# Folding the squares to one tile on GpSimd and VectorE before TensorE averages them

## The chip, the core and the metric

The kernel runs on one core of a Trainium2 chip. The metric is the time of one execution on the device in microseconds (us), lower is better; for several executions the median is taken. The engines are TensorE (PE for matmuls, PEld for its weight loads), VectorE (DVE), ScalarE (ACT), GpSimd (POOL) and SyncE (SP), which issues the weight transfers. SBUF tiles and PSUM banks have 128 partitions.

## The reference

Two blocks of two layers each run on x of 256 tokens by 2048 features, in fp32. The first block's layers mix by windowed means (layer 0) or by a gated linear recurrence (layer 1), and add a gated embedding. The second block's layers (2 and 3 in the kernel) run three branches: latent attention, a spatial gate, and gated linear attention (gla) with 4 heads of 256 value columns. Every matmul is preceded or followed by a root-mean-square norm; those of x and of each gla head matter here:

```python
def rms_norm(x, g):
    xf = x.astype(jnp.float32)
    y = xf * lax.rsqrt(jnp.mean(xf * xf, axis=-1, keepdims=True) + EPS)
    return (y * g.astype(jnp.float32)).astype(x.dtype)
...
    h = rms_norm(x, norm_g)
    proj = h @ w_in
...
    o = o.transpose(1, 0, 3, 2, 4).reshape(B, S, GLA_HEADS, GLA_DV)
    o = rms_norm(o, o_g).astype(v.dtype)
```

## The kernel before

Activations lie with features on the partitions and the 256 tokens along the free dimension, so a tile of 128 features is 128x256. Weights stream in units of eight 128x128 tiles (512 KB) through four slots. ScalarE rounds a unit to w_hi (L896), VectorE makes the rest w_lo (L1278), and TensorE multiplies w_hi with the high and low part of x (L536, L537) and w_lo with the high part (L544); x is split the same way into xs. In stages "by token" the roles are turned (L566, L574). ScalarE and VectorE prepare a unit three units ahead of TensorE.

The norms are applied late: a stage multiplies un-normed x, and the result is multiplied by rstd. For that the mean of the squares over the features is needed, a sum over partitions. mean_square (L578) has TensorE multiply a constant 128x128 tile mean_d (each value 1/2048) with each tile of squares, one after another into ms_bank, in plain fp32. Behind it ScalarE takes the root (root, L968, with a table load where another function was loaded), VectorE the reciprocal (norm, L1290), and the result scales the products.

Six times x is fed into a stage (the "feeds" 0 to 5: window, gate of layer 0, conv, gate of layer 1, gqk of layer 2, gqk of layer 3). ScalarE squares x in four blocks of 128x1024. GpSimd adds them into sq_sum (4 tiles of 256; sum_squares, L1971). For feeds 0 to 4 it then folds sq_sum from four tiles to two (128x512, L1976). For feed 5 the adds stand in the stage wo of layer 2 (L2109, L2113) without a fold. TensorE averages two tiles (four for feed 5), behind unit 13 or 15 of the feed (mean_of_x).

In layers 2 and 3 the gla heads, the spatial gate and the attention run beside the large stages as side work: generators on each engine that yield the number of a unit, counted from the start of the stage latent, and go on once the engine has come to it. TensorE runs what is yielded as v between the high and the low products of unit v + 1. The other engines run it at unit v, behind the split of the unit three ahead. With scored_at(n) = 4 + 6n, head h has its output made by TensorE at scored_at(2h+2) - 2 (26 for head 1), squared by ScalarE into g_sq (two tiles, L1005) at scored_at(2h+2) - 1, averaged at max(scored_at(2h+2), 20) (20, 28, 40, 52), its root taken at max(scored_at(2h+2) + 1, 21) (21, 29, 41, 53), and normed by VectorE at 22 for head 0, else at min(scored_at(2h+3) - 1, 54) (33, 45, 54). gla_normed, counted there, is waited for by TensorE ahead of the scores of the next head, and by the attention sums at 59.

## Time and profile before

| | before |
|---|---|
| runs, us | 3332.09, 3361.66, 3338.16 |
| median, us | 3338.16 |
| profiled execution, us | 3333.02 |
| its span, us | 3331.2 |
| mean granted TensorE clock | 0.997 |
| TensorE busy | 3310.4 us, 99% |
| VectorE busy | 2290.7 us, 69% |
| ScalarE busy | 1670.7 us, 50% |
| GpSimd busy | 839.1 us, 25% |

The span is the time from the first to the last instruction of the profiled execution; the time of that execution is 1.8 us longer. Busy times are sums of the instructions' spans. Matmuls overlap in the trace, so what one occupies is read from the distance of starts. A timeline merges like instructions that follow each other, and gives the start, the time to the last one's end, the engine, the line, the operation, what it writes and reads, how many, and in brackets the idle time ahead and what ended it.

### The profile page before, as it was taken

How to read it: one execution, taken by the hardware profiler on the slowest of the kernel's cores; microseconds unless marked ns; L12 is line 12 of the kernel's file. 1: busy time of each engine (PE TensorE's matmuls, PEld its weight loads, DVE VectorE, ACT ScalarE, POOL GpSimd, SP SyncE). 2: the span in 40 equal slices, each digit the busy share in tenths (PEclk: the TensorE clock that was granted, in tenths of full speed). 3: DMA queues.
4: the chain of work that ended last, by engine and by line, in shares of the span. 5: the costliest groups of instructions: out<-in, count | busy, mean ns of one | idle time of the engine just before them, and what ended most of it. 6: DMA issues, size and time to landing. Idle time of an engine off the chain costs nothing.

```text
span 3331.2 us, 65552 instructions
## 1 busy us (share of the span) xinstructions
PE 3310.4 (99%) x27820; PEld 3264.4 (98%) x27820; DVE 2290.7 (69%) x3014; ACT 1670.7 (50%) x2108; POOL 839.1 (25%) x807
## 2 busy tenths in 40 slices
PE   9999999999999999999999999999999999999999
PEld 9999999999999999999899999999988999999999
DVE  6986654688888845778878755555567777555554
ACT  5344444555588745555544444444455545444443
POOL 1532320144556500423323200000013232100000
PEclk9999999999999999999999999999999999999999
DMA  6565565556555565555444555555554444555555
GB/s 228 188 203 190 196 224 191 171 173 220 191 181 186 197 224 178 188 172 177 158 165 158 166 192 195 196 192 194 194 179 157 165 151 157 192 191 196 195 192 178
DMA packets 170051, 619.73 MB, mean 186 GB/s; under 512 B 19104, under 2 KB 20768, under 8 KB 169376
## 3 DMA queue, kind: packets, MB, share of 16 engines
q1 hardware_dynamic: 165888, 602.23, 54.6%
q10 hardware_dynamic: 3872, 13.31, 1.1%
q8 instruction: 220, 3.60, 0.4%
q14 instruction: 71, 0.58, 0.1%
HBM read 610.22 MB, written 4.19 MB: 184 GB/s over the span
## 4 chain that ended last, share of the span: by engine, by line
PE 90%; DVE 4%; ACT 4%; issue 1%; DMA 0%; ACTq 0%; SPq 0%; DVEq 0%
PE banks L544 21%; PE banks L536 21%; PE banks L537 21%; PE banks L566 4%; PE pm L544 3%; PE pm L536 3%; PE pm L537 3%; PE banks L574 2%; PE banks L601 2%; PE banks L603 2%; PE banks L608 2%; ACT w_hi L896 2%; DVE w_lo L1278 2%; PE pm L601 1%; PE pm L603 1%; PE pm L608 1%
## 5 line engine op out<-in xcount | busy, mean ns | idle before, releaser
L1278 DVE TENSOR_TENSOR w_lo<-raw,w_hi 128x1024 fp32r<-128x1024 f32 x1144 | 1467.6, 1287 | 868.9 <-ACT w_hi L896 857.0
L896 ACT ACTIVATE w_hi<-raw 128x1024 fp32r<-128x1024 f32 x1144 | 1204.7, 1057 | 974.4 <-PE banks L544 665.6
L536 PE MATMUL banks<-xs,w_hi 128*128 128x256 f32 x4008 | 948.2, 279 | 0.3 <-ACT val L1162 0.3
L537 PE MATMUL banks<-xs,w_hi 128*128 128x256 f32 x4008 | 947.4, 278 | 0.0
L536 PEld LDWEIGHTS banks<-xs,w_hi 128*128 128x128 f32 x4008 | 758.3, 189 | 0.9 <-ACT val L1162 0.7
L537 PEld LDWEIGHTS banks<-xs,w_hi 128*128 128x128 f32 x4008 | 758.3, 189 | 0.2
L544 PE MATMUL banks<-xs,w_lo 128*128 128x256 f32 x4008 | 550.6, 279 | 0.0
L544 PEld LDWEIGHTS banks<-xs,w_lo 128*128 128x128 f32 x4008 | 498.5, 189 | 0.4
L536 PE MATMUL pm<-xs,w_hi 128*128 128x256 f32 x952 | 223.1, 277 | 0.0
L537 PE MATMUL pm<-xs,w_hi 128*128 128x256 f32 x952 | 222.7, 276 | 0.0
L1937 POOL CAST merged<-act 128x256 fp32r<-128x256 f32 x32 | 41.0, 1281 | 714.7 <-DVE act L1717 714.7
L536 PE MATMUL banks<-inner,w_hi 128*128 128x256 f32 x896 | 211.2, 276 | 0.0
L537 PE MATMUL banks<-inner,w_hi 128*128 128x256 f32 x896 | 211.0, 276 | 0.0
L537 PEld LDWEIGHTS pm<-xs,w_hi 128*128 128x128 f32 x952 | 178.9, 188 | 0.1
L536 PE MATMUL banks<-y_abc,w_hi 128*128 128x256 f32 x768 | 178.9, 276 | 0.0
L536 PEld LDWEIGHTS pm<-xs,w_hi 128*128 128x128 f32 x952 | 178.8, 188 | 0.1
L537 PE MATMUL banks<-y_abc,w_hi 128*128 128x256 f32 x768 | 178.8, 276 | 0.0
L537 PEld LDWEIGHTS banks<-inner,w_hi 128*128 128x128 f32 x896 | 168.3, 188 | 0.0
L536 PEld LDWEIGHTS banks<-inner,w_hi 128*128 128x128 f32 x896 | 168.2, 188 | 0.0
L537 PEld LDWEIGHTS banks<-y_abc,w_hi 128*128 128x128 f32 x768 | 144.2, 188 | 0.0
L536 PEld LDWEIGHTS banks<-y_abc,w_hi 128*128 128x128 f32 x768 | 144.2, 188 | 0.0
L1178 ACT ACTIVATE act<-val 128x256 f32<-128x256 f32 x96 | 40.1, 417 | 197.4 <-DVE val L1704 197.4
(336 smaller groups left out, 5922.4 us busy)
## 6 DMA issues: line engine op xcount, KB each, us to landing
raw<-weights SPq DMA_DIRECT2D x1144, 512.0 KB, 3.4
wide<-x_in ACTq DMA_DIRECT2D x4, 512.0 KB, 8.9
wide<-x_in ACTq DMA_DIRECT2D x1, 2048.0 KB, 8.4
x_scratch<-wide ACTq DMA_DIRECT2D x1, 2048.0 KB, 9.1
wide<-x_scratch ACTq DMA_DIRECT2D x1, 2048.0 KB, 10.6
out_x<-wide SPq DMA_DIRECT2D x3, 512.0 KB, 5.3
w_st<-w_s ACTq DMA_DIRECT2D x2, 512.0 KB, 4.2
b_st<-b_s ACTq DMA_DIRECT2D x2, 512.0 KB, 5.6
```

Of the source, the lines that this page charges most:

```text
L536: nc.tensor.matmul(bank, w_hi[:, slot, w], x[:, 0:T], start=(k + t == 0), stop=False)
L537: nc.tensor.matmul(bank, w_hi[:, slot, w], x[:, T:2 * T], start=False, stop=False)
L544: ins = nc.tensor.matmul(bank, w_lo[:, slot, w], p.operand(i, k + t)[:, 0:T], start=False, stop=(k + t == p.depth - 1))
L566: nc.tensor.matmul(product_bank(s, i, j), x[:, at:at + P], w_hi[:, slot, w], start=(k == 0 and at < T), stop=False)
L574: ins = nc.tensor.matmul(product_bank(s, i, j), x[:, j * P:(j + 1) * P], w_lo[:, slot, w], start=False, stop=(k == depth - 1))
L601: nc.tensor.matmul(bank, w_hi[:, slot, w], operand[:, k, 0:T], start=(k == 0 and j < 4), stop=False, skip_group_check=True)
L603: nc.tensor.matmul(bank, w_hi[:, slot, w], operand[:, k, T:2 * T], start=False, stop=False, skip_group_check=True)
L608: ins = nc.tensor.matmul(bank, w_lo[:, slot, w], operand[:, k, 0:T], start=False, stop=(k == s.products[0].depth - 1), skip_group_check=True)
L896: nc.scalar.activation(w_hi[:, slot, :], raw[:, slot, :], ACT.Copy).then_inc(hi_done, 1)
L1178: nc.scalar.activation(act[:, slot, :], val[:, 2 * slot, :], ACT.Tanh, scale=0.5).then_inc(act_ready, 1)
L1278: nc.vector.tensor_tensor(w_lo[:, slot, :], raw[:, slot, :], w_hi[:, slot, :].bitcast(F32), ALU.subtract).then_inc(lo_done, 1)
L1937: link(nc.gpsimd.tensor_copy(dest[:, 0:T], source))
```

## The change

Three edits. On GpSimd a new function fold_squares folds sq_sum from four tiles to two and from two to one, behind the sums of feeds 0 to 4 and now of feed 5 too. On VectorE an add of 128x256 folds the two tiles of g_sq to one for each gla head, at scored_at(2h+2), behind ScalarE's square, and counts gla_folded, for which TensorE waits in place of gla_sq. TensorE averages one tile in all these places. For heads 1 to 3 TensorE's average and ScalarE's root are yielded one unit later than before, and VectorE's norm of head 3 at 55 and not at 54.

```diff
@@ mean_of_x
-                        mean_square(s.layer, which, [sq_sum[:, j, :] for j in range(4 if f == 5 else 2)])
+                        mean_square(s.layer, which, [sq_sum[:, 0, :]])
@@ TensorE gla_results
-                    yield max(scored_at(2 * h + 2), 20)
-                    pe.wait_ge(gla_sq, c * G_HEADS + h + 1)
+                    yield max(scored_at(2 * h + 2) + 1, 20)
+                    pe.wait_ge(gla_folded, c * G_HEADS + h + 1)
                     if h == 1:
                         pe.wait_ge(tok_read, 2 * c + 2)
-                    mean_square(c + 2, f"gla{h}", [g_sq[:, 0, :], g_sq[:, 1, :]])
+                    mean_square(c + 2, f"gla{h}", [g_sq[:, 0, :]])
@@ ScalarE gla_results
-                    yield max(scored_at(2 * h + 2) + 1, 21)
+                    yield max(scored_at(2 * h + 2) + 2, 21)
                     root(c + 2, f"gla{h}", 2 * P, eps128_col)
@@ VectorE gla_results
-                    yield min(scored_at(2 * h + 3) - 1, 54) if h else 22
+                    yield scored_at(2 * h + 2)
+                    ve.wait_ge(gla_sq, c * G_HEADS + h + 1)
+                    nc.vector.tensor_tensor(g_sq[:, 0, :], g_sq[:, 0, :], g_sq[:, 1, :], ALU.add).then_inc(gla_folded, 1)
+                    yield min(scored_at(2 * h + 3) - 1, 55) if h else 22
                     norm(c + 2, f"gla{h}", g_rstd)
@@ GpSimd
                 link(ins)
-                nc.gpsimd.tensor_tensor(sq_sum[:, 0:2, :], sq_sum[:, 0:2, :], sq_sum[:, 2:4, :], ALU.add)\
+                fold_squares()
+
+            def fold_squares():
+
+                link(nc.gpsimd.tensor_tensor(sq_sum[:, 0:2, :], sq_sum[:, 0:2, :], sq_sum[:, 2:4, :], ALU.add))
+                nc.gpsimd.tensor_tensor(sq_sum[:, 0, :], sq_sum[:, 0, :], sq_sum[:, 1, :], ALU.add)\
                     .then_inc(sq_summed, 1)
@@ GpSimd, feed 5
                         ins = nc.gpsimd.tensor_tensor(sq_sum, sq_sum, block_[:, :, :], ALU.add)
-                        ins.then_inc(sq_used if b == 2 else sq_summed, 1)
+                        if b == 2:
+                            ins.then_inc(sq_used, 1)
+                    link(ins)
+                    fold_squares()
```

The new code stands one line or more further down, so the lines of the same instruction differ by one on TensorE (L582 is L583 in the changed kernel) and by a few elsewhere.

TensorE around the average of head 1 in layer 2, in the stage by token vb, before (L658 are products of the gla scores):

```order
L574 MATMUL banks<-w_lo,xs 128x512 x4
L566 MATMUL banks<-w_hi,xs 128x512 x8
L658 MATMUL pm<-g_q,g_d 128x64 x8
L582 MATMUL ms_bank<-g_sq,mean_d 128x256 x2
L574 MATMUL banks<-w_lo,xs 128x512 x4
L566 MATMUL banks<-w_hi,xs 128x512 x8
L574 MATMUL banks<-w_lo,xs 128x512 x4
```

The same place in the changed kernel:

```order
L575 MATMUL banks<-w_lo,xs 128x512 x4
L567 MATMUL banks<-w_hi,xs 128x512 x8
L659 MATMUL pm<-g_q,g_d 128x64 x8
L575 MATMUL banks<-w_lo,xs 128x512 x4
L567 MATMUL banks<-w_hi,xs 128x512 x8
L583 MATMUL ms_bank<-g_sq,mean_d 128x256
L575 MATMUL banks<-w_lo,xs 128x512 x4
```

The average has one product and not two, and stands in the next unit.

VectorE around the fold of head 0 in layer 2, during the stage latent, in the changed kernel (before, the same rows stand without the row that writes g_sq; L1279 is the split into w_lo, L1401 the decay differences):

```order
L1684 TENSOR_TENSOR val<-banks,rstd_x 128x256
L1401 TENSOR_TENSOR g_d<-b_cum 128x256 x2
L1752 SCALAR_TENSOR_TENSOR latent<-val,chan,latent 128x256
L1279 TENSOR_TENSOR w_lo<-raw,w_hi 128x1024
L1475 TENSOR_TENSOR g_sq<-g_sq 128x256
L1401 TENSOR_TENSOR g_d<-b_cum 128x256 x2
L1279 TENSOR_TENSOR w_lo<-raw,w_hi 128x1024 x2
```

The fold comes behind one w_lo and ahead of the differences and the next w_lo.

GpSimd at the end of the sums for feed 5, in the changed kernel (before, the two folds L1984 and L1985 are not there):

```order
L2118 TENSOR_TENSOR sq_sum<-val,act 128x1024
L2122 TENSOR_TENSOR sq_sum<-sq_sum,val 128x1024
L2122 TENSOR_TENSOR sq_sum<-sq_sum,act 128x1024
L1984 TENSOR_TENSOR sq_sum<-sq_sum 128x512
L1985 TENSOR_TENSOR sq_sum<-sq_sum 128x256
L2003 MEMSET acc_kv 128x256
L2008 MEMSET acc 128x256
```

Two adds stand between the last sum and the memsets.

## Rows read from the trace of the kernel before

**Rows 1.** The page, busy us (share of the span) and instructions by engine
```profile
PE 3310.4 (99%) x27820; PEld 3264.4 (98%) x27820; DVE 2290.7 (69%) x3014; ACT 1670.7 (50%) x2108; POOL 839.1 (25%) x807
```
**Rows 2.** Waits of TensorE: us in total, times, longest (the largest of seven)
```profile
PE banks L544 <- DVE w_lo L1278: 6.1, 12, 0.5
```
**Rows 3.** Line 582 alone: duration ns min/median/max, first and last start us
```profile
L582 PE MATMUL ms_bank<-g_sq,mean_d x32: 377/379/436, 1596.3 to 2650.7; 128*128 128x256 f32 x32
L582 PE MATMUL ms_bank<-sq_sum,mean_d x28: 377/378/381, 50.5 to 2417.3; 128*128 128x256 f32 x28
```
**Rows 4.** Timeline of TensorE, units by token of layer 2: start us, us
```profile
1585.76 1.99 PE L566 MATMUL banks<-w_hi,xs 128*128 128x512 f32 x8
...
1588.51 1.99 PE L566 MATMUL banks<-w_hi,xs 128*128 128x512 f32 x8
1590.34 0.59 PE L582 MATMUL ms_bank<-acc_kv,mean_d 128*128 128x256 f32 x2
...
1591.68 1.99 PE L566 MATMUL banks<-w_hi,xs 128*128 128x512 f32 x8
...
1594.43 2.00 PE L566 MATMUL banks<-w_hi,xs 128*128 128x512 f32 x8
1596.27 1.03 PE L582 MATMUL ms_bank<-g_sq,mean_d 128*128 128x256 f32 x4
...
1598.07 1.99 PE L566 MATMUL banks<-w_hi,xs 128*128 128x512 f32 x8
```
**Rows 5.** Timeline of TensorE at the averages of feeds 0, 1 and 5
```profile
50.51 1.02 PE L582 MATMUL ms_bank<-sq_sum,mean_d 128*128 128x256 f32 x4
51.18 0.47 PE L601 MATMUL banks<-xs,w_hi 128*128 128x256 f32 x1
...
678.44 1.02 PE L582 MATMUL ms_bank<-sq_sum,mean_d 128*128 128x256 f32 x4
...
2415.77 1.89 PE L582 MATMUL ms_bank<-sq_sum,mean_d 128*128 128x256 f32 x8
2417.31 0.47 PE L601 MATMUL banks<-xs,w_hi 128*128 128x256 f32 x1
```
**Rows 6.** Timeline of GpSimd at the end of the sums, feeds 1 and 5
```profile
673.75 2.15 POOL L1976 TENSOR_TENSOR sq_sum<-sq_sum 128x512 f32<-128x512 f32 x1
...
2404.52 2.51 POOL L2113 TENSOR_TENSOR sq_sum<-sq_sum,act 128x1024 f32<-128x1024 f32 x1 [13.81 <-ACT act L918]
...
2417.78 0.31 POOL L1999 MEMSET acc<- 128x256 f32 x1 [10.50 <-PE ms_bank L582]
```
**Rows 7.** Adds on GpSimd by tile: duration ns min/median/max, first and last start
```profile
L1971 POOL TENSOR_TENSOR sq_sum<-sq_sum,act x10: 2445/3290/6411, 24.0 to 1463.5; 128x1024 f32<-128x1024 f32 x10
...
L1976 POOL TENSOR_TENSOR sq_sum<-sq_sum x5: 2152/2157/2158, 41.3 to 1466.8; 128x512 f32<-128x512 f32 x5
...
L2038 POOL TENSOR_TENSOR acc<-acc,val x32: 737/745/1052, 460.5 to 1315.9; 128x256 f32<-128x256 f32 x32
L2044 POOL TENSOR_TENSOR acc<-acc,sq x28: 1588/1620/1688, 691.9 to 1421.0; 128x256 f32<-128x256 f32 x28
```
**Rows 8.** VectorE's instructions that write g_d, columns as in rows 7
```profile
L1400 DVE TENSOR_TENSOR g_d<-b_cum x64: 405/415/1505, 1522.6 to 2610.1; 128x256 f32<-128x256 f32 x64
```
**Rows 9.** Timelines of ScalarE and VectorE around head 0's square, layer 2
```profile
1579.09 0.58 ACT L1005 ACTIVATE g_sq<-pm 128x512 f32<-128x512 f32 x1
...
1581.86 0.75 DVE L1400 TENSOR_TENSOR g_d<-b_cum 128x256 f32<-128x256 f32 x2
1582.53 1.22 DVE L1278 TENSOR_TENSOR w_lo<-raw,w_hi 128x1024 fp32r<-128x1024 f32 x1
1587.11 1.23 DVE L1278 TENSOR_TENSOR w_lo<-raw,w_hi 128x1024 fp32r<-128x1024 f32 x1 [3.36 <-ACT w_hi L896]
```
**Rows 10.** Timelines of ScalarE and VectorE: head 1's root and reciprocal, layer 2
```profile
1625.81 0.47 ACT L968 ACTIVATE rms<-ms_bank,power 128x256 f32<-128x256 f32 x1 [2.06 <-PE ms_bank L582]
...
1640.62 1.73 DVE L1290 RECIPROCAL g_rstd<-rms 128x256 f32<-128x256 f32 x1
```

More of the change, by code:

```diff
@@ L285, in build @@
             sem("att_rep"), sem("att_roped"))
+        gla_folded = sem("gla_folded")
         q_turned, q_cleared, q_moved, att_scores, att_max, att_exp, att_probs, att_turned, att_pt, att_o, att_done = (
```

## The prediction, made before the changed kernel ran

> **What bounds the kernel now.** I read the page's busy times first, then the list of waits for TensorE alone, then the groups on the line of the averaging matmuls, and last the timelines of each engine around the places that the diff touches. In the busy times the reader is to see TensorE at 99% of the span, VectorE at 69%, ScalarE at 50% and GpSimd at 25% [rows 1]. In the waits of TensorE the largest entry is 6.1 us in twelve pieces of at most 0.5 us, for w_lo; no entry names sq_sum or g_sq [rows 2]. So TensorE's queue is the path from end to end. A matmul taken out of it shortens the run by what it occupies, unless something else then makes TensorE wait.
>
> **What goes.** mean_square issues one product in plain fp32 for each tile of squares. In the trace one such product is two MATMUL records: 8 heads by 2 tiles appear as 32 records, and the six feeds (5 by 2 tiles, 1 by 4) as 28 [rows 3]. After the change there is one tile each, so 8 products go with the heads, 5 with the feeds 0 to 4, and 3 with feed 5: 16 products, 32 records.
>
> What one occupies cannot be read from the record's length (377 ns), since records overlap; it is read from starts. In the stages by token a unit without side work runs from 1585.76 to 1588.51, 2.75 us. The unit with one product (latent norm) runs from 1588.51 to 1591.68, 3.17 us. The unit of head 0 with two runs from 1594.43 to 1598.07, 3.64 us [rows 4]. One product costs 0.42 us, two cost 0.89, so the second costs 0.47. In the feeds, two products start at 50.51 and the next matmul at 51.18, that is 0.67 us; the four of feed 5 start at 2415.77 and the next matmul at 2417.31, that is 1.54 us [rows 5]. Two products more cost 0.87 us, 0.435 each. The two readings agree on 0.42 to 0.47 us for a product, and what it costs to enter and leave this work doesn't depend on the count.
>
> The sum: 8 x 0.47 = 3.76 for the heads, 5 x 0.435 = 2.18 for feeds 0 to 4, 3 x 0.435 = 1.31 for feed 5, together 7.2 us. With 0.42 throughout it is 6.7. I take **7.0 us**, with 6.7 and 7.5 (16 x 0.47) as ends.
>
> The Trainium skill (FP8 and Floating Point Precision, TensorE Precision Notes) says that true fp32 takes four passes through the array; by that the estimate is four times 256 columns for each product. Its page on the trace (Perfetto Trace Analysis, Identifying the Most-Contended Engine) halves the output rate for FP32_LOW_HIGH; read as half rate for a whole product and not for each record it would make each worth only some 0.21 us and the gain 3.4 us. The starts in the timeline speak for the four passes, and the sum above goes by them alone.
>
> **What is added on GpSimd.** Feeds 0 to 4 get one add of 128x256 behind the fold of 128x512; feed 5 gets both folds. The trace has no add of 128x256 on sq_sum. From below: half of the 128x512 fold's 2.15 us, 1.08 [rows 6], and the adds of val into acc, 0.74 [rows 7]. From above: the add of sq into acc, 1.59 to 1.69 us [rows 7]. In contention the 128x1024 add went from 2.45 to 6.41 us [rows 7], 2.6 times, which would make 2.8 us of 1.08. I take 1.1, the row nearest in kind. It is free where the result still comes before TensorE asks. Feed 1 (gate of layer 0) is the tightest: the fold ends at 673.75 + 2.15 = 675.90, and TensorE begins its average at 678.44, 2.5 us later. With 1.1 us and the link between, 1.4 us are left; with 1.69, 0.8; with 2.8, TensorE waits 0.3. In feed 5 the last add ends at 2404.52 + 2.51 = 2407.03; 2.15 + 1.1 more make it 2410.3, against 2415.77 [rows 5, 6]: over 5 us left. Behind these folds GpSimd's next work waits for TensorE anyway (the memset of acc waits 10.50 us in feed 5 [rows 6]). Cost zero; without that cover, 5 x 1.1 + 3.3 = 8.8 us.
>
> The Trainium skill (GPSIMD Engine Reference, Engine selection) says to put an elementwise add on VectorE, GpSimd being about twice as slow with two inputs. Its Key points add that the two engines contend for SBUF when VectorE reads two SBUF inputs. The trace agrees on the second: the same shape took 2.45 and 6.41 us [rows 7]. It changes the margin of feed 1 and not the place of the work.
>
> **What is added on VectorE.** Eight adds of 128x256. The nearest row is the difference into g_d, the same shape with the same two kinds of operand: 405 ns at least, 415 in the median, 1505 at most, where GpSimd works beside it [rows 8]. So 8 x 0.42 = 3.3 us of VectorE, at most 12, on an engine that is idle 31% of the span. At head 0 the fold goes ahead of the differences at 1581.86. The w_lo split behind it starts at 1582.53, and the next one waits 3.36 us for ScalarE [rows 9]: the idle time takes it up. That w_lo ends near 1583.75 and belongs to the unit that TensorE begins at 1591.68 [rows 4] (unit 20 counted as the side work counts), so VectorE leads by nearly 8 us. Cost on the path zero; uncovered 3.3 us, at most 12.
>
> The fold adds a wait on VectorE, for ScalarE's square. Queued behind it are the differences of the decay and w_lo, for which TensorE waits. For head 0 the square starts at 1579.09 and takes 0.58, so it ends at 1579.67, 2.2 us before the fold's place at 1581.86 [rows 9]: no wait. On the other heads the fold has the same distance in units (square at unit 12h+15, fold at 12h+16).
>
> **What is moved.** For heads 1 to 3 the average moves one unit later on TensorE and the root one unit later on ScalarE; for head 0 both keep their place (the maxima 20 and 21 still rule). The root is followed by a long pause: for head 1 the root starts at 1625.81 and takes 0.47, while the reciprocal that reads it starts at 1640.62 [rows 10], 14.3 us later, and its place in VectorE's order does not move. One unit, 2.75 us, goes into that pause. On ScalarE the two decay steps of head 1 now stand ahead of the root, and the table load between them moves ahead of the root; the order of the change has the same number of table loads. Head 3's reciprocal moves from 54 to 55, one unit; TensorE needs it at the attention sums, yielded at 59. No DMA is added or moved past.
>
> **The sum.** The profiled execution took 3333.02 us, its span 3331.2. Less 7.0 this is 3326.0, with a span of 3324.2. The timed runs of before are 3332.09, 3338.16 and 3361.66, so the profiled execution lies 5.1 us under their median and near their lowest. A median of new runs will rather lie above the sum than below it; I add 2 for that and say 3328.
>
> **The rivals.**
> *The time is taken up elsewhere.* TensorE comes earlier and meets a late w_lo, as it does 12 times now [rows 2]. For it: VectorE gets more work and TensorE less. Against: those waits are 6.1 us together and no average stands among them; the gain is spread over 14 places of 0.43 us (1.3 at feed 5), each small against the lead of nearly 8 us. Of the 7 us between 0 and 4 would be left: 3329 to 3333, up to 3338 on the median.
> *A late fold.* At feed 1 the GpSimd add in contention passes TensorE's average. It starts to cost from an added 2.5 us; at 2.8 it costs 0.3 us. In feed 5 both folds stretched 2.6 times take 8.4 us, and 8.7 lie between 2407.03 and 2415.77. For it: one add in the rows was stretched so. Against: the fold of 128x512 never was, its least and most are 2152 and 2158 ns [rows 7]. The time would be 3326.3, as a median 3328. It does not change the sign.
> *Slower: the added step puts a unit into the chain of each head.* Square, fold, average, root, reciprocal, and then the next head's scores wait for gla_normed. If the reciprocal had to wait for the moved root and TensorE for it, each of the six moved heads would cost 2.75 us, 16.5 in all, less 7.0: 3342.5. The point from which it decides is a root more than 14 us late, or VectorE held at the fold by a square that comes 2.2 us later; and then nearly 8 us of lead must go before TensorE waits. The rows of before show these margins open; for it speaks only that nothing in them shows the new wait itself.
> *The change does not do what it says*, that is products stay: excluded by the order of instructions, which has one product where there were two or four.
>
> **How the numbers follow.** Forecast (6.7 to 7.5 us gone, nothing late) 0.82; taken up in part or whole 0.12; late fold at feed 1 0.03; slower by the chain 0.03. The range takes the sum's ends less the 0.9 by which the lowest run lies under the profiled one (3333.0 - 7.5 - 0.9 = 3324.6), with room to 3322 for scatter, and above the median's level with no gain (3338.2) and a little of the slower case, 3342. A median lifted by a run such as 3361.66 lies outside. 1% is 33 us, about what a measurement of this kernel tells from no change; all cases lie within it, so the same gets 0.97.
>
> **What the profile after would show.** The line of mean_square has 16 records on g_sq and 12 on sq_sum. The unit of head 0 is 3.17 us long. In feed 5 the next matmul starts 0.4 us or less behind the average. The waits of TensorE for w_lo stay near 6.1 us, and none is for sq_sum or g_sq. GpSimd's fold of 128x256 takes 1.1 us and feed 1 keeps over a microsecond. VectorE's fold takes 0.42 us. The prediction is wrong if the span falls by less than 4 or more than 9 us, or if TensorE waits at an average, or if w_lo waits grow by what the products saved.

## The result and the profile after

The changed kernel took 3355.81 us in the median of 21 runs (3332.46 to 3379.27), the kernel before 3336.16 us in 21 runs on the same chip (3325.91 to 3382.83). The ratio is 1.0038, with a 95% interval of 1.0020 to 1.0056: slower by 0.4%, some 13 us by the ratio and 20 by the medians. I had forecast 3328 us and a range that ends at 3342. The sign was wrong and the time lies outside the range. Measured against the 1% that I had set for telling a change, the two are the same, which the forecast gave 0.97; only the 21 runs of each kernel tell them apart. Single runs overlap: 4 of the 21 of the changed kernel are under 3341 us, and 4 of the 21 of before are over 3357. Its profiled execution took 3357.76 us, against 3333.02 before.

The page of the changed kernel, its span and busy times:

```profile
span 3356.0 us, 65503 instructions
PE 3340.1 (100%) x27788; PEld 3296.8 (98%) x27788; DVE 2294.3 (68%) x3022; ACT 1670.5 (50%) x2108; POOL 858.7 (26%) x814
```

TensorE has 32 records fewer than in [rows 1], as planned, and its busy time rose by 29.7 us. The waits of TensorE, the largest (us in total, times, longest):

```profile
PE banks L602 <- DVE xs L1308: 4.4, 4, 1.8
PE pm L626 <- DVE gated L1671: 4.0, 2, 2.0
...
PE banks L545 <- DVE w_lo L1279: 1.1, 2, 0.5
```

The wait for w_lo fell from the 6.1 us of [rows 2] to 1.1. No average waits. All waits of TensorE in this view together fell as well, from 18.1 to 12.9 us. So the time did not go into a new wait. It went into work that is the same in both kernels. The view of TensorE by windows shows it (columns: window, its length, busy us, number of matmul records, granted clock, DMA share, GB/s). The kernel before:

```profile
100.00:600.00 500.00, 500.00 (x4414) 1.00 0.60 199
850.00:950.00 100.00, 100.00 (x885) 1.00 0.58 188
960.00:1140.00 180.00, 173.91 (x1507) 1.00 0.55 184
1150.00:1300.00 150.00, 150.00 (x1326) 1.00 0.65 218
1950.00:2050.00 100.00, 100.00 (x885) 1.00 0.59 196
```

The changed kernel:

```profile
100.00:600.00 500.00, 500.00 (x4248) 1.00 0.56 192
850.00:950.00 100.00, 100.00 (x851) 1.00 0.56 185
960.00:1140.00 180.00, 178.88 (x1520) 1.00 0.54 182
1150.00:1300.00 150.00, 149.98 (x1273) 1.00 0.61 209
1950.00:2050.00 100.00, 100.00 (x885) 1.00 0.57 194
```

From 100 to 600 us both kernels run the same matmuls, of 128x256, with no idle time, at a granted clock of 1.00, which is the 2.4 GHz level. Before, 4414 of them start in 500 us, one every 113.3 ns. After it is 4248, one every 117.7 ns. These are two steady paces and not a scatter: 100 us hold 885 records at one and 851 at the other, and little between for hundreds of us. What the other engines do beside it does not set the pace: before, VectorE is busy 97 us of the 100 from 100 us on and 46 of those from 500 us on, and TensorE starts 885 matmuls in both. The second is not new: the kernel before has it too, ahead of feed 0.

The starts show where the pace changes. TensorE before, ahead of and behind the two products of feed 0 (the average of [rows 5] that starts at 50.51), in the timeline (start us, us):

```profile
49.69 0.28 PE L608 MATMUL banks<-xs,w_lo 128*128 128x256 f32 x1
49.80 0.40 PE L608 MATMUL pm<-xs,w_lo 128*128 128x256 f32 x2
...
50.27 0.40 PE L608 MATMUL pm<-xs,w_lo 128*128 128x256 f32 x2
...
51.61 0.28 PE L601 MATMUL banks<-xs,w_hi 128*128 128x256 f32 x1
...
51.85 0.28 PE L601 MATMUL pm<-xs,w_hi 128*128 128x256 f32 x1
...
52.30 0.28 PE L601 MATMUL banks<-xs,w_hi 128*128 128x256 f32 x1
...
52.65 0.28 PE L603 MATMUL banks<-xs,w_hi 128*128 128x256 f32 x1
```

The same place in the changed kernel, with its one product:

```profile
48.61 0.39 PE L609 MATMUL banks<-xs,w_lo 128*128 128x256 f32 x2
48.84 0.39 PE L609 MATMUL pm<-xs,w_lo 128*128 128x256 f32 x2
49.06 0.59 PE L583 MATMUL ms_bank<-sq_sum,mean_d 128*128 128x256 f32 x2
49.30 0.47 PE L602 MATMUL banks<-xs,w_hi 128*128 128x256 f32 x1
49.61 0.28 PE L604 MATMUL banks<-xs,w_hi 128*128 128x256 f32 x1
...
50.20 0.28 PE L602 MATMUL pm<-xs,w_hi 128*128 128x256 f32 x1
50.32 0.28 PE L604 MATMUL pm<-xs,w_hi 128*128 128x256 f32 x1
```

Before, the seven steps from 49.69 to the average at 50.51 take 0.82 us, 117 ns each, and behind it the seven from 51.85 to 52.65 take 0.80, 114 ns each: two products turned a slow stream into a fast one. In the changed kernel the four steps from 48.61 to 49.06 are 113 ns each, and behind the average the six from 49.61 to 50.32 take 0.71, 118 ns each. So the one product there ended a fast stream, and the slow one that followed lasted until about 645 us.

The rows of an average outside the feeds give the landmarks. Line 583 in the changed kernel by tile (columns as in rows 3):

```profile
L583 PE MATMUL ms_bank<-g_sq,mean_d x16: 377/378/382, 1625.0 to 2679.7; 128*128 128x256 f32 x16
L583 PE MATMUL ms_bank<-sq_sum,mean_d x12: 377/377/378, 49.1 to 2445.3; 128*128 128x256 f32 x12
L583 PE MATMUL ms_bank<-acc,mean_d x8: 377/378/378, 646.3 to 2557.7; 128*128 128x256 f32 x8
```

The kernel before:

```profile
L582 PE MATMUL ms_bank<-acc,mean_d x8: 377/378/378, 625.8 to 2529.7; 128*128 128x256 f32 x8
```

**The working.** At feed 0 the changed kernel is 1.4 us ahead (49.1 against 50.5). At the first average of acc it is 20.5 us behind (646.3 against 625.8). In between lie 21.9 us. The pace accounts for them: 500/4248 less 500/4414 us is 4.4 ns for each matmul; 575.3 us at 113.3 ns, less the average itself, are some 5070 matmuls, and 5070 x 4.43 ns is 22.4 us; less 0.4 for the product taken out, 22.0. The second slow stretch, from about 801 to 1346 us, brings the distance to 30.5 us at the second average of acc (1348.5 against 1318.0); at head 0 it is 28.7 (1625.0 against the 1596.3 of [rows 3]). It costs only where TensorE has no wait: from 960 to 1140 us the kernel before starts fewer matmuls (1507 against 1520), since it runs fast into a late w_lo. The rest comes from laying the two streams side by side: apart from the averages of the feeds and the heads, both hold 27760 matmul records (27820 less 60, and 27788 less 28), in the same order. Behind head 0 the distance falls to 27.4 us. It rises by 1.9 us over 50 us of work (1700 to 1750 before, 1728 to 1778 after), where the granted clock is 0.97 before and 0.92 after, so this part is not of the pace. It then stays at 29.3 us up to feed 5. Feed 5 gives back 1.3 us, as forecast, and layer 3 gives 3.3, more than the 1.8 of its four heads. The span ends 24.8 us longer.

### The profile page after: what moved, and what is told of

The parts are those of the page before. It is cut to its first block, busy times and chain, and to the rows that moved or that the text cites. A ratio compares the mean times of both kernels' runs of the same rounds, so it can differ in the third digit from the quotient of the medians.

```text
span 3356.0 us, 65503 instructions
## 1 busy us (share of the span) xinstructions
PE 3340.1 (100%) x27788; PEld 3296.8 (98%) x27788; DVE 2294.3 (68%) x3022; ACT 1670.5 (50%) x2108; POOL 858.7 (26%) x814
## 4 chain that ended last, share of the span: by engine, by line
PE 96%; DVE 2%; ACT 1%; DMA 0%; issue 0%; SPq 0%; ACTq 0%; DVEq 0%
PE banks L545 22%; PE banks L537 22%; PE banks L538 22%; PE pm L545 4%; PE pm L538 4%; PE pm L537 4%; PE banks L567 4%; PE banks L575 2%; PE banks L602 2%; PE banks L604 2%; PE banks L609 2%; PE pm L602 1%; PE pm L604 1%; PE pm L609 1%; PE pm L659 1%; DVE w_lo L1279 1%
## 5 line engine op out<-in xcount | busy, mean ns | idle before, releaser
L1279 DVE TENSOR_TENSOR w_lo<-raw,w_hi 128x1024 fp32r<-128x1024 f32 x1144 | 1468.3, 1288 | 881.7 <-ACT w_hi L897 866.6
L537 PE MATMUL banks<-xs,w_hi 128*128 128x256 f32 x4008 | 958.6, 280 | 0.3
L538 PE MATMUL banks<-xs,w_hi 128*128 128x256 f32 x4008 | 957.9, 280 | 0.0
L537 PE MATMUL pm<-xs,w_hi 128*128 128x256 f32 x952 | 229.9, 281 | 0.0
L538 PE MATMUL pm<-xs,w_hi 128*128 128x256 f32 x952 | 229.5, 281 | 0.0
L537 PE MATMUL banks<-inner,w_hi 128*128 128x256 f32 x896 | 218.3, 281 | 0.0
L538 PE MATMUL banks<-inner,w_hi 128*128 128x256 f32 x896 | 218.2, 281 | 0.0
L1941 POOL CAST inner<-act 128x256 fp32r<-128x256 f32 x64 | 72.9, 1140 | 277.7 <-DVE act L1766 197.2
```

What stands on the lines that cost most here:

```text
L537: nc.tensor.matmul(bank, w_hi[:, slot, w], x[:, 0:T], start=(k + t == 0), stop=False)
L538: nc.tensor.matmul(bank, w_hi[:, slot, w], x[:, T:2 * T], start=False, stop=False)
L1279: nc.vector.tensor_tensor(w_lo[:, slot, :], raw[:, slot, :], w_hi[:, slot, :].bitcast(F32), ALU.subtract).then_inc(lo_done, 1)
L1941: link(nc.gpsimd.tensor_copy(dest[:, 0:T], source))
```

## The experiments

The theory, which the expectations call the theory of the gait (their word for the pace): what is issued at an fp32 average decides which of the two paces the stream behind it takes. The rivals: the added folds and moved steps cost the time, or the loss belongs to the edit at the heads. All times are medians, of 12 runs where nothing else is said, with the kernel before measured between them on the same chip (35, 29, 23 and 17 runs of it, in the order of the four values in the table). The ratio is estimated from the single runs, and differs a little from the quotient of the medians: a loss of 20 us by the medians is 15 to 17 by the ratio. One run of e6 took 4100.51 us, which nothing here explains; its ratio leaves that run out. Edits are shown against the changed kernel, those of e2, e3 and e5 against the kernel before. x is the number of TensorE's records from 100 to 600 us in the profiled execution.

| kernel | median us | before us | ratio (95%) | span us | x |
|---|---|---|---|---|---|
| e1_repeat | 3331.59 | 3335.42 | 0.9977 (0.9947 to 1.0006) | 3322.7 | 4415 |
| e2_feeds_one_tile | 3355.28 | 3335.42 | 1.0044 (1.0018 to 1.0069) | 3353.4 | 4248 |
| e3_gla_only | 3330.24 | 3335.42 | 0.9989 (0.9966 to 1.0013) | 3321.8 | 4414 |
| e4_feeds_only | 3357.32 | 3335.42 | 1.0051 (1.0031 to 1.0071) | 3350.0 | 4247 |
| e5_feed0_one_tile | 3358.14 | 3338.02 | 1.0052 (1.0022 to 1.0081) | 3351.5 | 4248 |
| e6_halves | 3355.33 | 3338.02 | 1.0046 (1.0016 to 1.0075) | 3355.2 | 4248 |
| e7_half_filler | 3353.33 | 3338.02 | 1.0023 (0.9994 to 1.0053) | 3349.5 | 4248 |
| e8_counts, one run | 3361.97 | 3338.02 | | 3360.2 | 4248 |
| e9_two_products | 3329.65 | 3338.77 | 0.9959 (0.9939 to 0.9979) | 3324.8 | 4415 |
| e10_pair_ahead | 3332.63 | 3338.77 | 0.9975 (0.9950 to 1.0000) | 3326.3 | 4415 |
| e11_fillers, one run | 3334.19 | 3338.77 | | 3332.4 | 4414 |
| e12_half_behind | 3327.94 | 3336.31 | 0.9966 (0.9949 to 0.9983) | 3322.2 | 4414 |

**e1_repeat**: all folds and moves of the change, and as many products as before, the added ones repeating the same product.

```diff
             def mean_square(l, which, source, again=0):
+                for _ in range(again):
+                    nc.tensor.matmul(ms_bank[:, 0:T], mean_d[:, :], source[0], start=True, stop=True)
...
+                        mean_square(s.layer, which, [sq_sum[:, 0, :]], 3 if f == 5 else 1)
...
+                    mean_square(c + 2, f"gla{h}", [g_sq[:, 0, :]], 1)
```

> The changed kernel with the folds, the waits and the moved steps kept, but TensorE issues as many products at each average as before the change: the averaged tile is multiplied once more ahead of it (three times more in feed 5), and the last product overwrites. The result is the same. Theory of the gait: in the traces of before and after, a matmul of 256 columns follows the last one either at about 113.3 ns or at about 117.7 ns, and keeps to one of the two over hundreds of us; behind an average of two records (one product) it goes at 117.7 (all six feeds of the changed kernel), behind four records it was 113 to 114 in four of five feeds of before. By it this run goes back to before: about 3336 us, with the matmuls between 100 and 600 us at 113.3 ns (some 885 in 100 us). Rival, that the folds on VectorE and GpSimd or the moved steps cost the time: it stays slow and pays the products again, 3355 + 7 = about 3362.

It is not slower than before (0.9977), and its span is 33 us shorter than that of the changed kernel, though it issues 16 products more. The folds on VectorE and GpSimd and the moved averages and roots cost at most 2 us on the path, by the end of the interval, 1.0006. This rules out the rival that they cost the time, and the "slower by the chain" of the prediction.

**e2_feeds_one_tile**: the kernel before, with one product in each feed and no fold added. The other tile (three in feed 5) is left out of the mean, so the result is not that of the reference; only the time counts.

```diff
-                        mean_square(s.layer, which, [sq_sum[:, j, :] for j in range(4 if f == 5 else 2)])
+                        mean_square(s.layer, which, [sq_sum[:, 0, :]])
```

> The kernel of before, where each of the six feeds averages only the first tile of sq_sum; the other one (three in feed 5) is left out of the mean, and no fold, wait or step is added or moved. Theory of the gait: one product behind each feed is enough, so 117.7 ns from feed 0 to the next break of the stream, and again from feed 2: some 15 us or more over before, 3350 to 3360. Rival, folds and moves: TensorE only loses 8 products of 0.43 us, so 3336 - 3.5 = about 3332.

Slower by 0.44%, with no work added anywhere: taking products out of TensorE is enough to lose some 20 us (15 by the ratio). Two of its 12 runs, at 3336, do not show the loss. From 850 to 950 us this kernel was fast (x885), though its stretch up to 600 was slow.

**e3_gla_only** and **e4_feeds_only**: the change at the heads alone, and at the feeds alone (e3 keeps `range(4 if f == 5 else 2)` and the fold to two tiles; e4 keeps two products for each head and no fold on VectorE).

```diff
-                    mean_square(c + 2, f"gla{h}", [g_sq[:, 0, :], g_sq[:, 1, :]])
+                    mean_square(c + 2, f"gla{h}", [g_sq[:, 0, :]])
```

> The kernel of before with the edit of the gla heads alone (VectorE's fold, the moved averages, roots and norm of head 3); the feeds are averaged as before. Theory of the gait: the stretches behind the heads are short, between other side work that breaks the stream, so the gain of 8 x 0.43 = 3.4 us stands within some us: 3330 to 3336. Rival, that the fold's wait on VectorE and the moved steps cost the time: over 3345.

> The changed kernel with the gla heads as before, that is the edit of the feeds alone: GpSimd's folds, one product for each feed. Theory of the gait: nearly all of the loss is here, 3350 to 3360. Rival, that VectorE's folds and the moved steps cost it: 3336 - 3.5 = 3332.

The whole loss comes with the feeds (1.0051, from 850 to 950 us x852). The heads alone lose nothing (0.9989); the span of e3 is 9.4 us under that of before in this pair of profiles, its interval reaches to no change.

**e5_feed0_one_tile**: of the kernel before, one product less in one place, feed 0, where the second tile is left out of the mean.

```diff
-                        mean_square(s.layer, which, [sq_sum[:, j, :] for j in range(4 if f == 5 else 2)])
+                        mean_square(s.layer, which, [sq_sum[:, j, :] for j in range(4 if f == 5 else 2 if f else 1)])
```

> The kernel of before, where feed 0 alone averages one tile (the other one is left out of its mean); all other averages as before. Theory of the gait: one product less, 0.43 us gained, and TensorE goes at 117.7 instead of 113.3 ns from 50 us to the next average at about 625 us, some 4900 matmuls by 4.4 ns = 21 us: 3336 + 21 = about 3357, wherever feed 0 would have left it in the fast gait. Rival, that the loss is spread over all places where the products were taken out: a sixth of it or less, about 3339.

One product of 0.43 us less makes the kernel slower by 0.5%: 20 us by the medians, 17 by the ratio. Of its 12 runs none is under 3351 us. The two windows of TensorE:

```profile
100.00:600.00 500.00, 500.00 (x4248) 1.00 0.58 192
850.00:950.00 100.00, 100.00 (x885) 1.00 0.59 192
```

The stream behind feed 0 is slow; behind the averages that kept their two products it is fast again. In this profile the stream was slow ahead of feed 0 as well, as in the kernel before; there two products turned it to fast, here one left it slow.

**e6_halves** and **e7_half_filler**: is it the number of records, or the length? e6 splits the one product of the changed kernel in two of 128 columns each (four records, as before the change, but half the length). e7 puts one product of 128 columns ahead of it.

```diff
+                    for at in (0, P):
+                        ins = nc.tensor.matmul(ms_bank[:, at:at + P], mean_d[:, :], source[0][:, at:at + P],
+                                               start=True, stop=True)
```

```diff
+                    nc.tensor.matmul(ms_bank[:, 0:P], mean_d[:, :], source[0][:, 0:P], start=True, stop=True)
```

> The changed kernel, where the average of each of the six feeds is made in two products of 128 columns (four records of some 110 ns, in all the time of one product of 256 columns); the heads as in the changed kernel. If it is the number of records behind which the gait is chosen, four bring the fast one as in before, and the gain of the change remains: 3336 - 7 = about 3329. If it is the time that the block occupies or how it ends, the gait stays at 117.7 ns: about 3355.

> The changed kernel, where in the six feeds a product of 128 columns, whose result is overwritten, goes ahead of the average (two records of some 110 ns, then two of 215); the heads as in the changed kernel. By the number of records (four): fast gait, 3336 - 7 + 6 x 0.22 = about 3330. By the time of the block: open, since 0.65 us lies between the 0.43 of the slow and the 0.86 of the fast case; if slow, 3356.

Both have x4248, the slow pace. Out of a fast stream four records don't keep it fast, so the number of records is not what decides; nor does a half ahead keep it. (In feeds 1 and 2 e6 came in slow, and its two halves were followed by the fast pace.) For e7 the interval of the whole kernel (0.9994 to 1.0053) reaches to no change, and 3 of its 12 runs lie under 3338 us; its verdict rests on the profile.

**e8_counts**: the changed kernel with 3, 3, 3, 5, 6 and 2 products in feeds 0 to 5.

```diff
+                        mean_square(s.layer, which, [sq_sum[:, 0, :]], (2, 2, 2, 4, 5, 1)[f])
```

> A map, for its profile alone: the changed kernel, where the average of feeds 0, 1 and 2 is issued as three products, that of feed 3 as five, of feed 4 as six and of feed 5 as two (the last one overwrites each time). Seen so far, coming from the fast gait: 1 product leads to the slow one, 2 keep the fast one, 4 (feed 5) lead to the slow one. If the count decides, feed 5 with two products keeps the fast gait from 2410 us on, where before it lost it; the others show whether 3, 5 and 6 keep it. If the place in the program decides, feed 5 goes slow with two as well and feeds 0 to 2 stay fast with three.

More is not better: three products in feed 0 ended a fast stream and left x4248. In feed 5, where four products (before) and one (changed kernel) were followed by the slow pace, two kept a fast stream; so it is what is issued that decides there, and not the place in the program. In the timeline of TensorE:

```profile
2450.28 0.59 PE L583 MATMUL ms_bank<-sq_sum,mean_d 128*128 128x256 f32 x2
2450.71 0.59 PE L585 MATMUL ms_bank<-sq_sum,mean_d 128*128 128x256 f32 x2
2450.95 0.47 PE L604 MATMUL banks<-xs,w_hi 128*128 128x256 f32 x1
...
2452.06 0.28 PE L604 MATMUL banks<-xs,w_hi 128*128 128x256 f32 x1
...
2452.40 0.28 PE L606 MATMUL banks<-xs,w_hi 128*128 128x256 f32 x1
```

The last four starts are 0.34 us for three steps, 113 ns each. The two averages start 0.43 us apart, which is the length of one product by itself.

**e9_two_products**: the change at the heads as it is; in the feeds the sums are folded to two tiles (new only in feed 5) and TensorE averages two.

```diff
-                        mean_square(s.layer, which, [sq_sum[:, 0, :]])
+                        mean_square(s.layer, which, [sq_sum[:, 0, :], sq_sum[:, 1, :]])
...
-                nc.gpsimd.tensor_tensor(sq_sum[:, 0, :], sq_sum[:, 0, :], sq_sum[:, 1, :], ALU.add)\
```

> The changed kernel, where the feeds average two tiles (GpSimd folds four to two, now for feed 5 too, and not to one); the heads keep one product. By the map of the runs so far, coming from the fast gait, only two full products keep it. So five feeds are as in before, feed 5 goes from four products to two and keeps the fast gait from there to the stage by token (some 57 us by 3.8%), and the heads keep their gain: 8 x 0.43 + 2 x 0.43 + 2.2 = 6.5 us under before, about 3330. Rival, that the heads' edit gives nothing (its interval held one) and feed 5 neither: about 3336, same as before.

Faster than the kernel before: 0.9959, interval 0.9939 to 0.9979. All 12 runs are under 3335 us; of the 23 runs of before beside them 6 are over 3355, about one slow stretch longer. That the pace makes this scatter of one and the same kernel is likely and not shown, since no such run was profiled. What is shown is that the program alone does not fix the pace: up to the average of feed 0 TensorE has the same instructions in the changed kernel and in e12, and its stream there is fast in the one and slow in the other (113 and 118 ns). In its profile it still was slow from 1150 to 1300 us (x1276).

**e10_pair_ahead**: e9 with a pair of products on acc, of no use to the result, at unit 11 of feeds 0 and 2. That is two units ahead of the average in feed 0 and four in feed 2, where the expectation says two for both.

```diff
+                    if f in (0, 2) and u == 11:
+                        wait(pe, root_ready, norms[s.layer, which])
+                        for _ in range(2):
+                            nc.tensor.matmul(ms_bank[:, 0:T], mean_d[:, :], acc[:, :], start=True, stop=True)
```

> The kernel of the run e9_two_products, with two more products on acc, whose results are overwritten, two units ahead of the averages of feeds 0 and 2: 1.7 us of TensorE added. If two products keep the fast gait and often turn the slow one into it, fewer executions go slow from 50 to 600 us: in before about a quarter of the runs lie at 3350 and above; here there should be one in twelve or none, and the median at 3331. If the share of such runs is set by something else, it stays a quarter.

3332.63 us, 3 us over e9, with one run of 12 over 3335. That is about what the expectation gave, but e9 has no such run without the pairs, so they are not shown to help. In the profile the pair in feed 0 turned a slow stream fast.

**e11_fillers**: the changed kernel with products of other lengths about the one, another in each feed: 128 columns behind; two of 128 ahead; two of 128 behind; 64 ahead; three of 128 ahead; 192 ahead.

```diff
             def mean_square(l, which, source, ahead=(), behind=()):
+                for n in ahead:
+                    nc.tensor.matmul(ms_bank[:, 0:n], mean_d[:, :], source[0][:, 0:n], start=True, stop=True)
...
+                for n in behind:
+                    ins = nc.tensor.matmul(ms_bank[:, T:T + n], mean_d[:, :], source[0][:, 0:n], start=True, stop=True)
```

> A map, for its profile alone: the changed kernel with one product for each feed, and shorter fp32 products beside it, whose results are overwritten or go to an unused half of the bank: feed 0 one of 128 columns behind it, feed 1 two of 128 ahead, feed 2 two of 128 behind, feed 3 one of 64 ahead, feed 4 three of 128 ahead, feed 5 one of 192 ahead. If the time of the block decides (two full products take 0.86 us), feeds 1 and 2 (0.43 + 0.44 us) keep the fast gait where they come from it; if it takes two products of 256 columns, none of the six keeps it.

Each place was seen once, so this only picks candidates. Read from the starts ahead of and behind each: out of a fast stream, 128 columns behind (feed 0, x4414) and 192 ahead (feed 5) kept it fast; two of 128 ahead (feed 1), 64 ahead (feed 3) and three of 128 ahead (feed 4) turned it slow. Feed 2 came in slow and stayed so with two of 128 behind. Feed 1 takes as long as two full products (0.43 + 0.44 us) and went slow, so the length alone does not decide.

**e12_half_behind**: the changed kernel, with 128 columns behind the one product in every feed.

```diff
+                for n in behind:
+                    ins = nc.tensor.matmul(ms_bank[:, T:T + n], mean_d[:, :], source[0][:, 0:n], start=True, stop=True)
...
+                        mean_square(s.layer, which, [sq_sum[:, 0, :]], (P,))
```

> The changed kernel with all its folds and one product for each feed, and behind it, in each of the six feeds, one product of 128 columns into an unused half of the bank (two records of 110 ns, 0.22 us; its result is read by nothing). In the run e11_fillers such a product behind the average of feed 0 was followed by the fast gait. If that holds everywhere, coming from the fast gait, six feeds cost 0.65 us each where two products cost 0.86, and the time is 3329.6 - 1.3 = about 3328.5 against 3336 of before. If feed 0 of that run was chance, about 3350 to 3355 as in the changed kernel.

3327.94 us, 0.9966 (0.9949 to 0.9983) of before; all 12 runs lie between 3323.29 and 3331.38 us, where the 17 of before beside them reach to 3359. It is the fastest of the kernels here by its median, and keeps every fold of the change. Against e9 (3329.65 beside other runs of before) it isn't told apart. Its feed 0 in the timeline of TensorE, and its windows:

```profile
49.59 0.40 PE L611 MATMUL pm<-xs,w_lo 128*128 128x256 f32 x2
49.83 0.60 PE L583 MATMUL ms_bank<-sq_sum,mean_d 128*128 128x256 f32 x2
50.26 0.38 PE L586 MATMUL ms_bank<-sq_sum,mean_d 128*128 128x128 f32 x2
50.40 0.37 PE L604 MATMUL banks<-xs,w_hi 128*128 128x256 f32 x1
50.60 0.28 PE L606 MATMUL banks<-xs,w_hi 128*128 128x256 f32 x1
```

```profile
100.00:600.00 500.00, 500.00 (x4414) 1.00 0.60 199
850.00:950.00 100.00, 100.00 (x885) 1.00 0.56 186
```

What the added product costs is read up to the second matmul behind it, since the first starts early beside an average: from the start of the average that is 0.77 us here (49.83 to 50.60), and 0.55 in the changed kernel (49.06 to 49.61). For 6 x 0.22 = 1.3 us of TensorE, 28 us are saved on the median of the changed kernel; by the ratios of both to the kernel before it is 24. In all six feeds the stream behind was fast, in four of them out of a slow one.

**The map.** The starts ahead of and behind the average of each feed, in all fourteen profiles (before, the changed kernel and the twelve runs), give this table. It says how often the stream behind was fast. Lengths count 0.43 us for a full product and 0.22 for one of 128 columns.

| issued at the average | length, us | out of a fast stream | out of a slow stream |
|---|---|---|---|
| one product | 0.43 | 0 of 14 | 3 of 5 |
| one, with 128 columns behind (e11, e12) | 0.65 | 3 of 3 | 4 of 4 |
| one, with 128 columns ahead (e7) | 0.65 | 0 of 6 | |
| two of 128 columns (e6) | 0.43 | 0 of 4 | 2 of 2 |
| two products | 0.86 | 24 of 24 | 7 of 8 |
| three products (e8) | 1.3 | 0 of 1 | 2 of 2 |
| four products | 1.7 | 0 of 4 | |
| five (e8) | 2.2 | 0 of 1 | |
| six (e8) | 2.6 | | 1 of 1 |

The other mixes of e11 were seen once each and are told there. Out of a fast stream each kind had the same outcome every time. Out of a slow one it had not: in e2 one product was followed by the slow pace in feed 0 and by the fast one in feeds 2 and 4.

**What stays open.** That the averages in the feeds set the pace is shown, by e5, e9, e12 and the map. Why is not. e7 and e12 issue products of the same length and the same number of instructions in the other order, and out of a fast stream the one goes slow and the other stays fast. They differ in one thing more: the added product of e12 writes an unused half of the bank, that of e7 the half of the average. Which of the two counts was not tried apart. So neither length nor number alone is the rule, nor a shift of the instructions that follow. In the trace a matmul's record is 276 ns long in the fast stream and 281 in the slow one, and of the weight loads between 100 and 600 us a third take 192 ns in the slow one (changed kernel) and none over 188 in the fast one (before); that names no cause. The pace also changes where no average stands: the changed kernel is fast again ahead of its average of acc at 646.3. What does that was not tried. One place is left unused: the single product on acc, at 625.8 and 1318.0 us in the kernel before, was followed by the slow pace all 28 times in the fourteen profiles, and no run changed it.

## Why the prediction was wrong

**Which products go, and what one occupies: right.** 16 records on g_sq and 12 on sq_sum are left, as forecast, where [rows 3] had 32 and 28. The unit of head 0 in the changed kernel:

```profile
1623.21 2.00 PE L567 MATMUL banks<-w_hi,xs 128*128 128x512 f32 x8
1625.04 0.60 PE L583 MATMUL ms_bank<-g_sq,mean_d 128*128 128x256 f32 x2
1625.29 1.28 PE L575 MATMUL banks<-w_lo,xs 128*128 128x512 f32 x4
1626.40 1.99 PE L567 MATMUL banks<-w_hi,xs 128*128 128x512 f32 x8
```

It takes 3.19 us (1626.40 - 1623.21), against 3.64 in [rows 4] and 3.17 forecast: 0.45 less for one product. In feed 5:

```profile
2445.06 0.59 PE L583 MATMUL ms_bank<-sq_sum,mean_d 128*128 128x256 f32 x2
2445.30 0.47 PE L602 MATMUL banks<-xs,w_hi 128*128 128x256 f32 x1
```

The next matmul follows 0.24 us behind the average, against 1.54 in [rows 5]: 1.30 for three products, as in the sum. So the 7 us are real. The half rate that the other reading of the Trainium skill would have given (0.21 for each) is excluded; the skill has that rate in Perfetto Trace Analysis, Engine Utilization, and not in the section that the prediction names.

**GpSimd: the price was too low, the cover held.** Its timeline at feed 1, the tightest:

```profile
692.59 2.16 POOL L1984 TENSOR_TENSOR sq_sum<-sq_sum 128x512 f32<-128x512 f32 x1
694.82 1.60 POOL L1985 TENSOR_TENSOR sq_sum<-sq_sum 128x256 f32<-128x256 f32 x1
```

and TensorE there:

```profile
697.32 0.59 PE L583 MATMUL ms_bank<-sq_sum,mean_d 128*128 128x256 f32 x2
```

The add takes 1.60 us where I took 1.1, the row "nearest in kind". It is the other one, acc with sq in [rows 7] (1.59 to 1.69), that it is like. It ends at 696.42, 0.9 us ahead of the average; I had forecast over a microsecond. The 6.41 us that I put down to contention with VectorE is not explained by it alone. In the kernel before an add of the same line took 3.29 us at 658.74, with VectorE busy all through; the one of 6.41 us had VectorE busy for 5.40 of 6.40; and the fold behind it took its usual 2.15 with VectorE busy all through.

**VectorE: right.** Its timeline at head 0:

```profile
1610.64 0.42 DVE L1475 TENSOR_TENSOR g_sq<-g_sq 128x256 f32<-128x256 f32 x1
...
1611.64 1.22 DVE L1279 TENSOR_TENSOR w_lo<-raw,w_hi 128x1024 fp32r<-128x1024 f32 x1
1615.89 1.23 DVE L1279 TENSOR_TENSOR w_lo<-raw,w_hi 128x1024 fp32r<-128x1024 f32 x1 [3.03 <-ACT w_hi L897]
```

The fold takes 0.42 us and waits for nothing, and the idle time ahead of the next w_lo goes from 3.36 us in [rows 9] to 3.03. The moved averages and roots cost nothing that e1 can tell.

**The step that failed** is the one the rest stood on: "A matmul taken out of it shortens the run by what it occupies, unless something else then makes TensorE wait." It takes the pace of all the other matmuls as fixed. The terms of the sum were sized well, and the sum left out a term three to four times as large: some 5070 matmuls in the first slow stretch, 4.4 ns each, are 22 us, and in all, by the medians, the 7 us gained and 20 lost make 27. None of my rivals had it. The one on the slower side gave 3342.5, 13 us under what came, by a chain that did not slow at all.

**What could have been seen.** Two signs lay in the profile of before. The starts ahead of the average of feed 0 are 117 ns apart and those behind 113 (x4414 in 500 us), and what sets this turn from low to high products apart from those of other units is the two products. And one of three timed runs was 3361.66 us, 23.5 over the median; I put it down as scatter, where it had the size of one slow stretch.

The Trainium skill (TensorE: Matmul & The Clock Gate, Back-to-back issue gap) gives one spacing at full clock for an isolated matmul of each size, 262 cycles for 256 columns; for a stream with weight loads it has values at 128 and 512 columns and none at 256. By the first, at 2.4 GHz, the estimate is 109 ns, for both kernels alike. The trace has two values for this size, both above it, 113.3 and 117.7 ns at a granted clock of 1.00. The same notes (Perfetto Trace Analysis, Identifying the Most-Contended Engine) send the reader to the busy share of the weight loads; here that is 98% in [rows 1] and 98% after, and can't tell the faster kernel from the slower. The count of records in equal windows can.

## What to carry to other kernels

Where one engine is the bound with no idle time, compare first how many of its instructions start in equal windows of the same work, before and after: a difference of 4% in a pace weighs more than any small operation that is taken out. A small edit in a long unbroken stream of matmuls can set the pace of thousands behind it; forecast it with a range as wide as one such stretch, here some 20 us. When an edit shortens such a stream and the time grows, put single instructions back one place at a time and look at the pace behind each. And when single runs of one kernel fall into two groups, look for two states of the bounding engine in the trace before calling it scatter.

## What was not expected of the hardware

TensorE runs the same stream of 128x256 matmuls at one of two steady paces, 113.3 or 117.7 ns from start to start (885 or 851 records in 100 us), at the same granted clock of 1.00 and with no wait, and holds it over 500 us and more. What stands at an fp32 average chooses between them: one product of 0.43 us less in feed 0 cost 17 to 20 us (e5), and 0.22 us more in each feed gained 24 to 28 us on the changed kernel (e12). Out of a fast stream one product was followed by the slow pace 14 times of 14, two by the fast one 24 of 24. On GpSimd the add of 128x256 took 1.60 us, three quarters of that of 128x512 (2.16 us) and not half; an add of 128x256 on other tiles took 0.74 [rows 7].
